# Two transformer blocks in split fp32: rows of the activations and slots of the weights 16 bytes longer

## The chip, the core and the metric

The kernel runs on one NeuronCore of a Trainium2 chip. The metric is the device time of one execution in microseconds (us). Matrix products run on TensorE (PE in the profile, its weight loads PEld), elementwise work on VectorE (DVE), ScalarE (ACT) and GpSimd (POOL); SyncE (SP) issues most DMAs. SBUF holds 128 partitions; a tensor `[P, k, t]` lies in each partition as k rows of t numbers of 4 bytes.

## What is computed

The reference chains two blocks on a stream x of 256 tokens and 1024 features, in float32:

```python
x = first_block(x, mem, ...)     # mixers of four kinds, cross-attention on mem, conv. gated FFN (2816)
return second_block(x, c, ctx, ...)
# second_block, two layers l:
x = ffn_half_step(x, mx[0:3], g_ffn1[l], ...)      # and the same for ctx
x = x + mx[5] * mixer(modulated_norm(x, ...))      # l = 0: Fourier and spatial gate; l = 1: attention over x and ctx
x = ffn_half_step(x, mx[6:9], g_ffn2[l], ...)      # and the same for ctx, in the first layer
# with
swiglu(h, w_gu, w_down) = (silu(h @ w_gate) * (h @ w_up)) @ w_down     # inner width 2752
ffn_half_step = x + 0.5 * gate * swiglu(rms_norm(x, g) * (1 + scale) + shift, ...)
```

Where x and ctx run together there are 512 tokens, elsewhere 256.

## The kernel before

**Split products.** Each product of an activation with a weight matrix is computed in three passes of a reduced-precision fp32 type (F32R, which TensorE takes in one pass at full clock). Both operands are split into a high and a low part: `w_hi` and `w_lo` for the weights, `xn_hi` and `xn_lo` for the normalised activations, `h_hi` and `h_lo` for the hidden units of the feed-forward. `three_passes` (L254) issues high by high (L258), high weights by low activations (L259) and low weights by high activations (L260). Each `matmul` call is a load of the first operand, the stationary one (128 columns), and a stream of the second, the moving one, of 256 or 512 columns. Products that are not split are plain fp32, which the profile shows as two matmul records for each call.

**Staging.** All weights are cut into chunks of at most 2048 columns by 128 partitions, 1 MB. SyncE loads them one after the other into the three slots of `raw`. For chunk g, ScalarE copies raw into `w_hi[:, g % 3]` (`split_hi`, L234), VectorE subtracts that from raw into `w_lo[:, g % 3]` (`split_lo`, L242), and TensorE waits for `lo_ready` before it uses the slot and raises `chunk_done` after it. Splits run two chunks ahead of the products.

**The loops on TensorE.** `pe_feature_major` goes through the chunks of a job; in each it goes over k (8 rows of the activations for an up or plain projection, 11 for a down projection) and within k over the output tiles n (two in general, one in the down projections). So six matmuls in a row share row k of the moving operand in an up projection, three in a down projection. A chunk is 48 matmuls in the one and 33 in the other. `win_pe` does the same for the input projections of the first block; its job `w_in_small` has one output tile. `pe_token_major` has the activations stationary and the weights moving. The job list is fixed in `plan`; the order on each engine is that of the program, with semaphores between engines.

**Where the tensors lie.** Tensors are allocated in the order in which they are named, each at the next multiple of 32 bytes: raw, w_hi, w_lo, xc, xn_hi, xn_lo, small, ident, minus, rot, row_sums, work, rstd, half, mods, gains, scales, b_mod, c_in, c_pad, mrow, and then those of a stage: z and the tables of the first block, later in the same place h_hi and h_lo, or the tensors of the two mixers of the second block. raw starts at a multiple of 64. `small` collects columns of constants and has 280 of them. `work` (8192 columns) is scratch; the feed-forward uses its columns 4096 to 7167, the norms 0 to 4095, the means of the last norm 7168 to 7679.

Of the kernel before, what the change touches and what calls it, by code (L numbers as in the profile page):

```python
# [38 lines left out]
F32 = mybir.dt.float32  # L39
F32R = mybir.dt.float32r  # L40
I32 = mybir.dt.int32
ACT = mybir.ActivationFunctionType
ALU = mybir.AluOpType
AX_X = mybir.AxisListType.X

P = 128
T = 256
D = 1024
KT = D // P
SLOTS = 3  # L50
CHUNK = 2048
EPS = 1e-6
HEADS = 4
HD = 64
FF_TILES = 22
HALF = FF_TILES // 2
# [72 lines left out]
def build(nc, io, plan):  # L129
# [23 lines left out]
    with ExitStack() as ctx:  # L153
        def sb(name, shape, dt=F32, scope=ctx):
            return scope.enter_context(nc.sbuf_tensor(name, shape, dt))
# [5 lines left out]


        raw = sb("raw", [P, SLOTS, CHUNK])
        w_hi = sb("w_hi", [P, SLOTS, CHUNK], F32R)
        w_lo = sb("w_lo", [P, SLOTS, CHUNK], F32R)
        xc = sb("xc", [P, KT, 2 * T])
        xn_hi = sb("xn_hi", [P, KT, 2 * T], F32R)
        xn_lo = sb("xn_lo", [P, KT, 2 * T], F32R)
        small = sb("small", [P, io["small"].shape[1]])
        ident = sb("ident", [P, P])  # L170
        minus = sb("minus", [P, P])
# [1 line left out]
        row_sums = sb("row_sums", [P, 32])  # L173
        work = sb("work", [P, 8192])
        nrm = work[:, 0:KT * 2 * T].rearrange("p (k t) -> p k t", k=KT)
        rstd = sb("rstd", [P, 2 * T])
        half = sb("half", [P, 2 * T])
        mods = sb("mods", [P, 144, 2])
# [2 lines left out]
        b_mod = sb("b_mod", [P, 144])  # L181
        c_in = sb("c_in", [P, KT, 2])
        c_pad = sb("c_pad", [P, KT, C_AT + 32])
        mrow = sb("mrow", [P, 256])
        X = slice(0, T)
        C = slice(T, 2 * T)
        XC = slice(0, 2 * T)
# [1292 lines left out]
            "ff_gate", "ff_hi", "ff_lo", "ff_convolved", "ff_newest_tap"))  # L1480
        later = ExitStack()
        mix.close()
        h_hi = sb("h_hi", [P, HALF, 2 * T], F32R, scope=later)
        h_lo = sb("h_lo", [P, HALF, 2 * T], F32R, scope=later)
        fbuf = [work[:, 4096 + i * 1024:4096 + (i + 1) * 1024].rearrange("p (n t) -> p n t", n=2) for i in range(SLOTS)]

        def packed(s):
# [487 lines left out]
        o_t = area(0, KT, 2 * T)  # L1975
# [64 lines left out]
        def branch_act(act, norm, then):  # L2040
            norm.act_rest(act)
            for name in L0_TABLES:
                act.dma_start(L0_TABLES[name][:], io[name]).then_inc(l0_tables_in, 16)
            run_act(act, jobs["ab_a"], act_copy_to(act, a_t, w=2 * T), counts=True)
            run_act(act, jobs["ab_v"], act_tokens_to(act, v_t, ACT.Gelu_apprx_tanh), counts=True)
            act.wait_ge(g_dve, 3)
            act.activation(vst2, vst, ACT.Abs_reciprocal_sqrt).then_inc(g_act, 1)
            run_act(act, jobs["ab_u"], act_copy_to(act, u_t, ACT.Gelu_apprx_tanh, w=2 * T), counts=True)

            def middle(j):  # L2050
                act.wait_ge(f_mid, j + 1)
                if j >= 2:
                    act.wait_ge(f_sum, j - 1)
                got, m, h = psum[:, MID_BANK + j % 2, 0:T].rearrange("p (n t) -> p n t", n=2), mid[j % 2], P // 2
                act.activation(m[:, :, 0:h + 1], got[:, :, 0:h + 1], ACT.Copy)
                act.activation(m[:, :, P + 1:P + h], got[:, :, h + 1:P], ACT.Copy)
                act.activation(m[:, :, P - 1:h:-1], got[:, :, 1:h], ACT.Copy)
                act.activation(m[:, :, 2 * P - 1:P + h:-1], got[:, :, h + 1:P], ACT.Copy, scale=-1.0).then_inc(f_mid_out, 1)

            def fourier_high(g):  # L2060
                act.wait_ge(f_sum_out, 4 * g + 4)
                act.activation(xn_hi[:, g, :], o_t[:, g, :], ACT.Copy).then_inc(o_hi, 1)

            def gated_high(i):
                act.wait_ge(g_dve, 10 + 2 * i)
                k = slice(4 + 2 * i, 6 + 2 * i)
                act.activation(xn_hi[:, k, :], o_t[:, k, :], ACT.Copy).then_inc(o_hi, 1)

            def odd_out(j):
                act.wait_ge(f_sum, j + 1)  # L2070
                if j >= 2:
                    act.wait_ge(f_sum_out, 2 * j - 2)
                act.activation(odd_half[j % 2], psum[:, TOKEN_BANK + j % 2, T:T + P + 1], ACT.Copy).then_inc(f_odd, 1)

            middle(0)
            for j in range(3):
                middle(j + 1)
                odd_out(j)
            fourier_high(0)
            middle(4)  # L2080
            odd_out(3)
            middle(5)
            odd_out(4)
            fourier_high(1)
            middle(6)
            odd_out(5)
            gated_high(0)
            middle(7)
            odd_out(6)
            fourier_high(2)  # L2090
            odd_out(7)
            gated_high(1)
            fourier_high(3)
            run_act(act, jobs["ab_out"], then.act_squares_after(act))

        def branch_dve(dve, rows_out, columns, closing):
            rows_out()
            run_dve(dve, jobs["ab_a"], None)
            columns()
            run_dve(dve, jobs["ab_v"], None)  # L2100
            n = 0

            def o(ins):
                nonlocal n
                n += 1
                ins.then_inc(g_dve, 1)
                dve.wait_ge(g_dve, n)
            v = v_t[:, :, :].rearrange("p n (g f) -> p (n g) f", f=P)
            dve.wait_ge(evacuated, jobs["ab_v"].base + 2)
            dve.wait_ge(l0_tables_in, 16 * len(L0_TABLES))  # L2110
            o(dve.tensor_tensor(vsq, v, v, ALU.mult))
            o(dve.tensor_reduce(vst3, vsq, AX_X, ALU.add))
            o(dve.tensor_scalar(vst, vst3, 1.0 / P, EPS, ALU.mult, ALU.add))
            dve.wait_ge(g_act, 1)
            o(dve.scalar_tensor_tensor(vst3, vst2, -0.5, vst2, ALU.mult, ALU.mult))
            o(dve.tensor_tensor(vst3, vst3, vst, ALU.mult))
            o(dve.scalar_tensor_tensor(vst2, vst3, 1.5, vst2, ALU.add, ALU.mult))
            o(dve.tensor_tensor(v, v, vst2.unsqueeze(2).to_broadcast([P, 16, P]), ALU.mult))
            gv = gv_row[:, :, :].unsqueeze(1).to_broadcast([P, 4, 4, P])
            v4 = v_t[:, :, :].rearrange("p n (g f) -> p n g f", f=P)  # L2120
            o(dve.tensor_tensor(v4, v4, gv, ALU.mult))
            for i in range(2):
                dve.memset(mid[i][:, :, P:2 * P:P // 2], 0.0).then_inc(f_clear, 1)
            run_dve(dve, jobs["ab_u"], None)

            def halves(j):

                dve.wait_ge(f_odd, j + 1)
                g, t = j // 2, j % 2 * T
                even, odd = psum[:, TOKEN_BANK + j % 2, 0:P + 1], odd_half[j % 2]  # L2130
                dve.tensor_tensor(o_t[:, g, t:t + P + 1], even, odd, ALU.add).then_inc(f_sum_out, 1)
                dve.tensor_tensor(o_t[:, g, t + T - 1:t + P:-1], even[:, 1:P], odd[:, 1:P], ALU.subtract).then_inc(f_sum_out, 1)

            def low(i, k):
                dve.wait_ge(o_hi, i + 1)
                dve.tensor_tensor(xn_lo[:, k, :], o_t[:, k, :], xn_hi[:, k, :].bitcast(F32), ALU.subtract).then_inc(o_lo, 1)

            def gated_sum(i):
                dve.wait_ge(g_pe, i + 1)
                gated = o_t[:, 4 + 2 * i:6 + 2 * i, :].rearrange("p g (n t) -> p g n t", t=P)  # L2140
                bs = bs_row[:, 2 * i:2 * i + 2, :].unsqueeze(2).to_broadcast([P, 2, 4, P])
                got = psum[:, GATED_BANK:GATED_BANK + 2, :].rearrange("p g (n t) -> p g n t", t=P)
                o(dve.tensor_tensor(gated, got, bs, ALU.add))

            def gated_product(i):
                k = slice(4 + 2 * i, 6 + 2 * i)
                o(dve.tensor_tensor(o_t[:, k, :], o_t[:, k, :], u_t[:, 2 * i:2 * i + 2, :], ALU.mult))

            for j in range(3):
                halves(j)  # L2150
            gated_sum(0)
            halves(3)
            gated_product(0)
            low(0, 0)
            halves(4)
            halves(5)
            low(1, 1)
            gated_sum(1)
            halves(6)
            gated_product(1)  # L2160
            low(2, slice(4, 6))
            halves(7)
            low(3, 2)
            low(4, slice(6, 8))
            low(5, 3)
            run_dve(dve, jobs["ab_out"], dve_add_gated(dve, 2, gate_of(1), 2), closing=closing.dve_last(dve, gate_of(1)))
# [45 lines left out]
        block = ctx.enter_context(nc.Block())  # L2212
# [743 lines left out]
```

## Time and profile before

| | |
|---|---|
| time, median of 3 runs | 2172.94 us (2171.1 to 2174.55) |
| span of the profiled execution | 2171.7 us |
| busy: TensorE, weight loads | 97%, 84% |
| busy: VectorE, ScalarE, GpSimd | 45%, 38%, 10% |
| granted TensorE clock, mean | 0.993 of full |
| DMA, mean | 145 GB/s |

A record of a matmul runs from its start to its modelled end, its latency included, so records of consecutive matmuls overlap. The pace of TensorE is read from the starts in the timeline. A stretch is described by its first and its last start and the number of intervals between them.

### The profile page before, as it was taken

Reading aid. Unit: us, or ns where it says so; the run is one execution under the profiler, and the core shown is the slowest. Engines: PE = TensorE matmul, PEld = TensorE weight load, DVE = VectorE, ACT = ScalarE, POOL = GpSimd, SP = SyncE. Lnnn points to the kernel's source line nnn. Section 1 sums busy time; section 2 is a strip of 40 time slices with the busy share of each in tenths; the row PEclk is TensorE's granted clock in tenths of the full one; section 3 lists DMA queues with packets and bytes.
Section 4 is the critical chain, followed back from the end, with each engine's and each line's share of the span. In section 5 each row is a group of like instructions: output and inputs, shape, how many; then the busy total and the mean of one; then the engine's idle time right before and its main releaser. Section 6 shows DMA issues by size and latency. Waiting matters only on the chain.

```text
span 2171.7 us, 31784 instructions
## 1 busy us (share of the span) xinstructions
PE 2104.7 (97%) x13882; PEld 1815.8 (84%) x13882; DVE 984.8 (45%) x1270; ACT 817.4 (38%) x1046; POOL 224.3 (10%) x185
## 2 busy tenths in 40 slices
PE   7988999999999999999999999999999999999998
PEld 6985998999878888788887888888778888869998
DVE  6768555767522322354542332243232235645444
ACT  5742455655522222244332222233222224445444
POOL 1000001413111010100101001111000110001001
PEclk9999999999999999999999999999999999999999
DMA  6425545454532333452343332243334222364453
GB/s 235 156 79 200 214 169 191 155 190 164 215 149 78 108 141 114 158 204 99 127 156 134 110 115 82 86 163 136 137 125 155 75 80 102 117 252 156 167 178 112
DMA packets 53708, 313.97 MB, mean 145 GB/s; under 512 B 5952, under 2 KB 12353, under 8 KB 23745
## 3 DMA queue, kind: packets, MB, share of 16 engines
q1 hardware_dynamic: 50848, 308.98, 39.7%
q10 hardware_dynamic: 2720, 2.95, 0.4%
q8 instruction: 109, 1.79, 0.3%
q14 instruction: 31, 0.25, 0.0%
HBM read 310.86 MB, written 1.05 MB: 144 GB/s over the span
## 4 chain that ended last, share of the span: by engine, by line
PE 86%; DVE 6%; ACT 4%; issue 3%; DMA 1%; SPq 0%; DVEq 0%; ACTq 0%
PE psum L258 26%; PE psum L260 26%; PE psum L259 26%; PE psum L1646 3%; ACT w_hi L234 2%; DVE w_lo L242 1%; PE psum L1293 1%; PE psum L1283 1%; PE psum L1307 0%; DMA raw<-in_w_in_r 0%; DVE xn_lo L1811 0%; PE psum L895 0%; PE psum L1714 0%; DVE work L1000 0%; PE psum L896 0%
## 5 line engine op out<-in xcount | busy, mean ns | idle before, releaser
L258 PE MATMUL psum<-xn_hi,w_hi 128*128 128x256 f32 (+1 forms) x2600 | 864.4, 332 | 17.5 <-DVE xn_lo L438 7.5
L259 PE MATMUL psum<-xn_lo,w_hi 128*128 128x256 f32 (+1 forms) x2600 | 853.2, 328 | 0.0
L260 PE MATMUL psum<-xn_hi,w_lo 128*128 128x256 f32 (+1 forms) x2600 | 852.8, 328 | 0.0
L242 DVE TENSOR_TENSOR w_lo<-raw,w_hi 128x2048 fp32r<-128x2048 f32 (+1 forms) x246 | 509.9, 2073 | 453.8 <-ACT w_hi L234 453.0
L258 PEld LDWEIGHTS psum<-xn_hi,w_hi 128*128 128x128 f32 x2600 | 497.0, 191 | 74.5 <-issue 23.3
L259 PEld LDWEIGHTS psum<-xn_lo,w_hi 128*128 128x128 f32 x2600 | 497.4, 191 | 43.0 <-issue 1.2
L260 PEld LDWEIGHTS psum<-xn_hi,w_lo 128*128 128x128 f32 x2600 | 497.2, 191 | 42.3
L234 ACT ACTIVATE w_hi<-raw 128x2048 fp32r<-128x2048 f32 (+1 forms) x246 | 421.7, 1714 | 216.9 <-PE psum L260 139.1
L258 PE MATMUL psum<-h_hi,w_hi 128*128 128x512 f32 (+1 forms) x913 | 314.9, 345 | 1.8 <-POOL h_lo L1621 1.7
L259 PE MATMUL psum<-h_lo,w_hi 128*128 128x512 f32 (+1 forms) x913 | 313.2, 343 | 0.0
L260 PE MATMUL psum<-h_hi,w_lo 128*128 128x512 f32 (+1 forms) x913 | 313.2, 343 | 0.0
L1621 POOL TENSOR_TENSOR h_lo<-work,h_hi 128x512 fp32r<-128x512 f32 (+1 forms) x110 | 154.4, 1404 | 1143.5 <-ACT h_hi L1553 1143.5
L1542 ACT ACTIVATE work<-psum 128x512 f32<-128x512 f32 (+1 forms) x88 | 47.9, 545 | 476.0 <-PE psum L260 476.0
L1591 DVE TENSOR_TENSOR work<-work,psum 128x512 f32<-128x512 f32 (+1 forms) x88 | 54.6, 621 | 373.0 <-ACT work L1542 373.0
L258 PEld LDWEIGHTS psum<-h_hi,w_hi 128*128 128x128 f32 x913 | 171.7, 188 | 27.0 <-issue 2.5
L259 PEld LDWEIGHTS psum<-h_lo,w_hi 128*128 128x128 f32 x913 | 171.8, 188 | 22.5
L260 PEld LDWEIGHTS psum<-h_hi,w_lo 128*128 128x128 f32 x913 | 171.8, 188 | 22.4
L1474 DVE SCALAR_TENSOR_TENSOR xc<-psum,mods,xc 128x256 f32<-128x256 f32 x126 | 55.7, 479 | 185.8 <-PE psum L260 185.5
L369 POOL TENSOR_TENSOR work<-work 128x256 f32<-128x256 f32 (+1 forms) x60 | 62.1, 1035 | 721.0 <-ACT work L360 671.6
L360 ACT ACTIVATE work<-xc 128x512 f32<-128x512 f32 (+2 forms) x42 | 26.1, 622 | 188.3 <-DVE xc L1474 167.0
L1553 ACT ACTIVATE h_hi<-work 128x512 fp32r<-128x512 f32 (+1 forms) x110 | 60.1, 546 | 81.4 <-DVE work L1591 81.4
L1646 PE MATMUL psum<-raw,c_pad 128*32 128x256 f32 x1152 | 73.6, 383 | 0.3 <-DMA raw<-in_mod 0.3
(375 smaller groups left out, 1324.4 us busy)
## 6 DMA issues: line engine op xcount, KB each, us to landing
raw<-in_mod SPq DMA_DIRECT2D x72, 1024.0 KB, 4.9
raw<-in_a_up SPq DMA_DIRECT2D x42, 1024.0 KB, 4.9
raw<-in_b_up SPq DMA_DIRECT2D x42, 1024.0 KB, 4.8
raw<-in_ffn_up SPq DMA_DIRECT2D x22, 1024.0 KB, 4.9
raw<-in_a_down SPq DMA_DIRECT2D x32, 704.0 KB, 4.1
raw<-in_b_down SPq DMA_DIRECT2D x32, 704.0 KB, 4.1
raw<-in_ffn_down SPq DMA_DIRECT2D x16, 704.0 KB, 4.2
raw<-in_wo SPq DMA_DIRECT2D x8, 1024.0 KB, 4.8
```

Of the source, the lines that this page charges most:

```text
L234: act.activation(w_hi[:, slot, 0:size], raw[:, raw_slot(("main", g)), 0:size], ACT.Copy).then_inc(hi_ready, 1)
L242: dve.tensor_tensor(w_lo[:, slot, 0:size], raw[:, raw_slot(("main", g)), 0:size], w_hi[:, slot, 0:size].bitcast(F32), ALU.subtract).then_i ...
L258: pe.matmul(out, lh, rh, start=first, stop=False, skip_group_check=group)
L259: pe.matmul(out, lh, rl, start=False, stop=False, skip_group_check=group)
L260: return pe.matmul(out, ll, rh, start=False, stop=last, skip_group_check=group)
L369: pool.tensor_tensor(nrm[:, 0, 0:self.w], nrm[:, 0, 0:self.w], nrm[:, k, 0:self.w], ALU.add).then_inc(n_added, 1)
L1474: mm = dve.scalar_tensor_tensor(x, got, gate[:, tile, h], x, ALU.mult, ALU.add)
L1542: act.activation(b[r, 0, 0:self.w], psum[r, s.bank, 0:self.w], ACT.Silu).then_inc(ff_gate, 1)
L1553: act.activation(out, b[r, 1:2, 0:self.w], ACT.Copy).then_inc(ff_hi, 1)
L1591: dve.tensor_tensor(b[r, 1, 0:self.w], b[r, 0, 0:self.w], up[up_r], ALU.mult).then_inc(evacuated, 1)
L1621: pool.tensor_tensor(lo, b[r, 1:2, 0:self.w], hi.bitcast(F32), ALU.subtract).then_inc(ff_lo, 1)
L1646: mm = pe.matmul(psum[q, 7, 0:256], c_pad[:, k, C_AT - 2 * j:C_AT - 2 * j + 32], raw[:, raw_slot(("mod", m)), k * 256:(k + 1) * 256], star ...
```

## The change

Four tensors of split operands get four more columns (16 bytes) in each row or slot. Nothing reads or writes these columns; where a whole row was addressed, a slice (`XC`, columns 0 to 511) takes its place. `small` is filled up with zero columns to a multiple of 16 columns. `mrow`, a buffer of 256 columns that turns the modulation rows into columns, is no tensor of its own any more but a part of `work`.

```diff
+ROW_PAD = 4
@@
-        w_hi = sb("w_hi", [P, SLOTS, CHUNK], F32R)
-        w_lo = sb("w_lo", [P, SLOTS, CHUNK], F32R)
+        w_hi = sb("w_hi", [P, SLOTS, CHUNK + ROW_PAD], F32R)
+        w_lo = sb("w_lo", [P, SLOTS, CHUNK + ROW_PAD], F32R)
         xc = sb("xc", [P, KT, 2 * T])
-        xn_hi = sb("xn_hi", [P, KT, 2 * T], F32R)
-        xn_lo = sb("xn_lo", [P, KT, 2 * T], F32R)
+        xn_hi = sb("xn_hi", [P, KT, 2 * T + ROW_PAD], F32R)
+        xn_lo = sb("xn_lo", [P, KT, 2 * T + ROW_PAD], F32R)
@@
         nrm = work[:, 0:KT * 2 * T].rearrange("p (k t) -> p k t", k=KT)
+        mrow = work[:, 7680:7936]
@@
-        mrow = sb("mrow", [P, 256])
@@
-        h_hi = sb("h_hi", [P, HALF, 2 * T], F32R, scope=later)
-        h_lo = sb("h_lo", [P, HALF, 2 * T], F32R, scope=later)
+        h_hi = sb("h_hi", [P, HALF, 2 * T + ROW_PAD], F32R, scope=later)
+        h_lo = sb("h_lo", [P, HALF, 2 * T + ROW_PAD], F32R, scope=later)
@@
-                act.activation(xn_hi[:, g, :], o_t[:, g, :], ACT.Copy).then_inc(o_hi, 1)
+                act.activation(xn_hi[:, g, XC], o_t[:, g, :], ACT.Copy).then_inc(o_hi, 1)
@@
-                act.activation(xn_hi[:, k, :], o_t[:, k, :], ACT.Copy).then_inc(o_hi, 1)
+                act.activation(xn_hi[:, k, XC], o_t[:, k, :], ACT.Copy).then_inc(o_hi, 1)
@@
-                dve.tensor_tensor(xn_lo[:, k, :], o_t[:, k, :], xn_hi[:, k, :].bitcast(F32), ALU.subtract).then_inc(o_lo, 1)
+                dve.tensor_tensor(xn_lo[:, k, XC], o_t[:, k, :], xn_hi[:, k, XC].bitcast(F32), ALU.subtract).then_inc(o_lo, 1)
@@
+    block("pad", np.zeros((P, -width % 16)))
```

## Rows read from the trace of the kernel before

**Rows 1.** The page's part 1: busy us, share of the span, instructions

```profile
PE 2104.7 (97%) x13882; PEld 1815.8 (84%) x13882; DVE 984.8 (45%) x1270; ACT 817.4 (38%) x1046; POOL 224.3 (10%) x185
```

**Rows 2.** The page's part 4: the chain that ended last, by line

```profile
PE psum L258 26%; PE psum L260 26%; PE psum L259 26%; PE psum L1646 3%; ACT w_hi L234 2%; DVE w_lo L242 1%; PE psum L1293 1%; PE psum L1283 1%; PE psum L1307 0%; DMA raw<-in_w_in_r 0%; DVE xn_lo L1811 0%; PE psum L895 0%; PE psum L1714 0%; 
```

**Rows 3.** Waits of TensorE: total us, times, longest us; the largest

```profile
PE psum L373 <- POOL work L369: 9.1, 1, 9.1
```

**Rows 4.** Groups by form: line engine op out<-in shapes xcount | busy us, mean ns | idle

```profile
L258 PE MATMUL psum<-xn_hi,w_hi 128*128 128x256 f32 x1520 | 442.7, 291 | 17.5 <-DVE xn_lo L438 7.5 <-DVE xn_lo L1811 4.0 <-DVE xn_lo L440 3.7
L258 PE MATMUL psum<-xn_hi,w_hi 128*128 128x512 f32 x1080 | 421.7, 390 | 0.0
L258 PE MATMUL psum<-h_hi,w_hi 128*128 128x512 f32 x495 | 196.4, 397 | 0.0
L258 PE MATMUL psum<-h_hi,w_hi 128*128 128x256 f32 x418 | 118.6, 284 | 1.8 <-POOL h_lo L1621 1.7
L258 PE MATMUL psum<-w_hi,xn_hi 128*128 128x256 f32 x160 | 46.7, 292 | 0.0
```

**Rows 5.** Timeline of TensorE: start us, us, line; 256 columns on xn, 44 rows

```profile
2009.82 0.28 PE L258 MATMUL psum<-xn_hi,w_hi 128*128 128x256 f32 x1
...
2014.98 0.28 PE L259 MATMUL psum<-xn_lo,w_hi 128*128 128x256 f32 x1
```

**Rows 6.** The same view, 512 columns on xn, 49 rows

```profile
1318.54 0.39 PE L258 MATMUL psum<-xn_hi,w_hi 128*128 128x512 f32 x1
...
1329.42 0.39 PE L258 MATMUL psum<-xn_hi,w_hi 128*128 128x512 f32 x1
```

**Rows 7.** The same view, 256 columns on h, 33 rows

```profile
535.73 0.28 PE L260 MATMUL psum<-h_hi,w_lo 128*128 128x256 f32 x1
...
539.51 0.28 PE L259 MATMUL psum<-h_lo,w_hi 128*128 128x256 f32 x1
```

**Rows 8.** The same view, 512 columns on h, 35 rows

```profile
692.01 0.40 PE L259 MATMUL psum<-h_lo,w_hi 128*128 128x512 f32 x1
...
699.94 0.40 PE L260 MATMUL psum<-h_hi,w_lo 128*128 128x512 f32 x1
```

**Rows 9.** The same view, w_in_small, 22 rows

```profile
64.19 0.28 PE L258 MATMUL psum<-xn_hi,w_hi 128*128 128x256 f32 x1
...
66.71 0.28 PE L258 MATMUL psum<-xn_hi,w_hi 128*128 128x256 f32 x1
```

**Rows 10.** The same view at the halved clock, 22 rows, and its granted clock

```profile
122.37 0.41 PE L260 MATMUL psum<-xn_hi,w_lo 128*128 128x256 f32 x1
...
126.85 0.41 PE L260 MATMUL psum<-xn_hi,w_lo 128*128 128x256 f32 x1
...
122.00:127.00 5.00, 5.00 (x24) 0.50 0.32 98
```

**Rows 11.** The same view, fp32 products of the attention, eight in one row

```profile
1898.69 1.89 PE L1293 MATMUL psum<-work,v 128*128 128x256 f32 x8
```

**Rows 12.** Instructions of line 1293: duration ns min/median/max, first and last start

```profile
L1293 PE MATMUL psum<-work,v x64: 379/379/483, 1898.7 to 1942.9; 128*128 128x256 f32 x64
```

**Rows 13.** Timeline of TensorE where 512 columns begin, rows 1, 2, 3 and 6

```profile
958.02 0.40 PE L258 MATMUL psum<-xn_hi,w_hi 128*128 128x512 f32 x1
958.25 0.40 PE L259 MATMUL psum<-xn_lo,w_hi 128*128 128x512 f32 x1
958.49 0.39 PE L260 MATMUL psum<-xn_hi,w_lo 128*128 128x512 f32 x1
...
959.18 0.39 PE L260 MATMUL psum<-xn_hi,w_lo 128*128 128x512 f32 x1
```

**Rows 14.** The same view where 256 columns begin, rows 1 and 10

```profile
2069.86 0.28 PE L258 MATMUL psum<-xn_hi,w_hi 128*128 128x256 f32 x1
...
2070.93 0.28 PE L258 MATMUL psum<-xn_hi,w_hi 128*128 128x256 f32 x1
```

**Rows 15.** Splitting on VectorE, by form; columns as in rows 4

```profile
L242 DVE TENSOR_TENSOR w_lo<-raw,w_hi 128x2048 fp32r<-128x2048 f32 x161 | 370.4, 2301 | 333.9 <-ACT w_hi L234 333.3
```

## The prediction, made before the change was run

> **What bounds the kernel now.** I read the shares first, then the clock and the chain, then the starts of single matmuls. TensorE is busy for 2104.7 of 2171.7 us, VectorE for 45% of the span and ScalarE for 38% [rows 1]. The chain that ended last lies 26% each on the lines 258, 259 and 260, the three passes of the split product [rows 2]; the longest waits of TensorE together are a few tens of us, the largest 9.1 us [rows 3]. So the time is the number of matmuls times the interval between their starts, and almost nothing else. The counts per pass are in [rows 4]: with the activations as moving operand 1520 of 256 columns and 1080 of 512, with the hidden units 418 and 495, and 160 with the weights moving. Times three passes that makes 5040 matmuls of 256 columns and 3240 of 512 on the normalised activations, 1254 and 1485 on the hidden units.
>
> The mean durations in [rows 4] are of no use for an interval, since a matmul's record covers its latency as well. The reader has to take starts. Between 2009.82 and 2014.98 us lie 43 intervals, 120.0 ns each [rows 5]; between 1318.54 and 1329.42 lie 48, 226.7 ns each [rows 6]. On the hidden units, from 535.73 to 539.51, there are 32 intervals of 118.1 ns [rows 7] and from 692.01 to 699.94 there are 34 of 233.2 ns [rows 8].
>
> **Why phase can matter at all.** These four figures differ by operand, not only by size. The code gives the addresses. All tensors up to `small` have sizes that are multiples of 64 bytes; `small` has 280 columns, 1120 bytes, so all that comes after it, h_hi and h_lo among it, starts 32 bytes beyond a multiple of 64, while xn_hi, xn_lo, w_hi and w_lo start at one. Both rows and slots are 2048 and 8192 bytes, so k and slot change nothing. Hence moving and stationary operand have the same phase where xn is used, and phases 32 apart where h is used: 226.7 against 233.2 ns at 512 columns, 120.0 against 118.1 at 256. That the down projection fills one bank while the up projections alternate between two is not the reason: w_in_small also fills a single bank and its 21 intervals from 64.19 to 66.71 are 120.0 ns each [rows 9].
>
> What the ideal is shows where the moving operand is read at half the rate. At the halved clock (granted 0.50) the 21 intervals from 122.37 to 126.85 are 213.3 ns for 256 columns, which is 256 columns at 1.2 GHz with nothing on top [rows 10]. The unsplit fp32 products of line 1293 stream at the same rate at full clock: eight last 1.89 us of which the last takes 0.379 [rows 11, 12], so 1.511/7 = 215.9 ns, 2.6 on top, although their operands have mixed phases. At full rate 256 and 512 columns last 106.7 and 213.3 ns at 2.4 GHz; the overheads are then 13.3 and 13.4 ns with equal phases and 11.4 and 19.9 with phases 32 apart. So some 9 to 17 ns of every split matmul are a stall that comes only when the moving operand is streamed at full rate beside the next weight load.
>
> The third thing to see is that the steady intervals are a state that is reached. When 512 columns begin at 958.02, the first five intervals are (959.18 - 958.02)/5 = 232.0 ns, and only then does it run at 226.7 [rows 13]; when 256 columns begin after the hidden units at 2069.86 the first nine are (2070.93 - 2069.86)/9 = 118.9 ns [rows 14], before 120.0 holds. Out of this locked state the equal phases therefore cost about the same as phases 32 apart: about 232 and 118.5.
>
> **The change, part by part.** Row k of xn_hi, xn_lo, h_hi and h_lo now lies at 16 times (k mod 4) bytes beyond a multiple of 64, slot s of the weights at 16 s. `small` grows to 288 columns (1152 bytes), and h starts at 0 instead of 32. In every chunk the difference of phase between moving and stationary operand therefore runs through 0, 16, 32 and 48 and moves on after six matmuls in the up projections (two tiles of three passes) and after three in the down projections.
>
> First the term of the order. The lock takes about five intervals to form [rows 13], and the phase moves on after three or six, so I take it that it no longer forms. For 512 columns on xn that costs 232.0 - 226.7 = 5.3 ns times 3240 = +17.2 us, less 0.5 us for the some hundred matmuls that are unlocked now (20 stretches of five). For 512 columns on h it gives (232.0 - 233.2) times 1485 = -1.8 us. For 256 columns on xn, 118.5 - 120.0 = -1.5 ns times 5040 = -7.6 us, less 0.7 that is unlocked now; on h (118.5 - 118.1) times 1254 = +0.5. The sum is 17.2 - 0.5 - 1.8 - 7.6 + 0.7 + 0.5 = +8.5 us. A sixth matmul of each six may run locked, which takes some 2 us off. I forecast +6 to +7.
>
> Then the term that the trace does not show: phases 16 and 48 apart, which half of the matmuls get. Its lower bound is the overhead of the half-rate stream, 2.6 ns [rows 11]: 109.3 and 215.9 ns, which against the forecast is (118.5 - 109.3) times 6294/2 = 29 us and (232.0 - 215.9) times 4725/2 = 38 us, together 67 us less than forecast. Its upper bound is the worst single interval shown, 240 ns in the starts of [rows 13] (958.25 to 958.49), 8 more than the forecast's; with the same 8 ns at 256 columns, 8 times (2362 + 3147) gives 44 us more. I take neither, since the two differences that are shown agree out of lock within 1.2 ns, and a difference of 16 lies between them.
>
> The skill has a rule against all of this. The Trainium skill, SBUF — State Buffer, section SBUF: two separate sides, says that only the port pair shared by VectorE and GpSimd causes contention and that TensorE never waits for anyone at its ports; TensorE: Matmul & The Clock Gate, section Step-by-step, adds that loading the next weights takes no read bandwidth from the running matmul. By these pages phase would be nothing and the change would cost nothing. [rows 6] and [rows 8] differ by 6.5 ns a matmul with the same count of columns, so the trace doesn't agree with the rule taken that far; what it would mean is the second rival.
>
> The other parts have one answer. Writers: the second half of splitting a chunk takes VectorE 2301 ns on average [rows 15], while the 48 matmuls of a chunk of 256 columns last 48 times 120, 5.76 us, so a few ns more or less of a write at phase 16 is hidden behind them; if that cover is gone, at the start of a stage, it counts. The chain has 3% in the two splits [rows 2], at the starts of stages; 1% of slower writes there is 0.6 us. `mrow` moves into columns of `work` that nothing else uses; its six copies and what waits for them stay as they are. The slices with `XC` cut the new padding off: the same elements in two runs. No instruction, DMA or wait is added on any queue; the DMA of `small` carries 32 bytes more in each of 128 rows. Identity, `minus`, `work` and z move from phase 32 to 0; their products are the half-rate ones, 2.6 ns on top whatever the phase.
>
> **The rivals.** (1) *The streams come apart, and it is faster.* If the stall is a meeting of the two read streams in the same 16 bytes modulo 64, then a difference of 16 or 48 may let one run ahead of the other without meeting. For it: the stall vanishes at half rate, and differences 0 and 32 are both even. Against: weights advance more slowly than the moving operand, so the two lap each other from any start. It decides the sign from 2 ns less in the odd rows: 2 times 5509 matmuls is 11 us, which turns +6 into -5. The full price is 67 us under the forecast, 2112; half of it, which I take, gives about 2145. (2) *Nothing changes.* The lock forms anew within a row or carries over, or the order of banks and not the phase makes the difference; time 2173. For it: 256 and 512 columns nearly cancel. (3) *Odd starts cost more*, as reads that straddle a unit of 32 bytes: up to 44 us over the forecast, 2195 at a middle price and 2222 at the full one. Nothing in the trace reads a split operand at such a start.
>
> **How the numbers follow.** The profiled span of 2171.7 us is within 1.3 us of the median, 2172.9, so I add to the median: 2172.9 + 6 = 2179. Chances: the forecast 0.42, faster by parting 0.28, nothing 0.15, odd starts cost more 0.15. A measurement can tell about 0.2%, 4.3 us, from no change. The forecast's own range, 2166 to 2190, splits into 0.09 below 2168.6, 0.13 within 0.2% and 0.20 above 2177.3. The second rival goes to no change but for 0.01. That gives faster 0.28 + 0.09 = 0.37, same 0.13 + 0.14 = 0.27, slower 0.20 + 0.15 + 0.01 = 0.36. The range leaves out the full prices of the first rival and of the third: 2132 to 2203.
>
> **What would show it.** Starts in the profile after: up chunks of 512 columns near 232 ns without runs of 226.7; chunks of 256 near 118.5; down chunks of 512 no longer in pairs of 232 and 235. If odd rows stand out within a chunk, with six intervals shorter or longer than their neighbours, the first or third rival holds, and that is what would make the prediction wrong by tens of us. If up chunks show 226.7 throughout, the lock does not depend on the difference. Busy TensorE should stay at 97%, the waits of [rows 3] as they are.

## The result, and the profile after

The changed kernel takes 2181.87 us (median of 5 runs, 2180.73 to 2184.43), the kernel before beside it 2173.32 us. The ratio is 1.0041, 95% interval 1.003 to 1.0051: slower, by 8.6 us. The forecast was 2179.0 us. The profiled execution spans 2179.1 us, 7.4 more than before.

First the shares, the chain and the longest wait of TensorE, which answer to [rows 1], [rows 2] and [rows 3]:

```profile
PE 2110.4 (97%) x13881; PEld 1809.4 (83%) x13882; DVE 985.5 (45%) x1270; ACT 818.2 (38%) x1046; POOL 225.7 (10%) x185
...
PE psum L259 26%; PE psum L260 25%; PE psum L261 25%; PE psum L1647 3%; ACT w_hi L235 2%; DVE w_lo L243 2%; PE psum L1294 1%; PE psum L1284 1%; DVE work L432 0%; PE psum L1308 0%; DMA raw<-in_w_in_r 0%; DVE xn_lo L1812 0%; PE psum L896 0%; DVE work L1001 0%; PE psum L897 0%
...
PE psum L374 <- POOL work L370: 8.8, 1, 8.8
```

Little but TensorE's own busy time moved: 2110.4 against 2104.7 us. The three passes (now lines 259 to 261) still carry the chain, and the longest wait is 8.8 us where it was 9.1. Next the groups by form, in the columns of [rows 4]:

```profile
L259 PE MATMUL psum<-xn_hi,w_hi 128*128 128x256 f32 x1520 | 440.4, 290 | 19.6 <-DVE xn_lo L439 8.7 <-DVE xn_lo L441 3.7 <-DVE xn_lo L1812 3.6
L259 PE MATMUL psum<-xn_hi,w_hi 128*128 128x512 f32 x1080 | 426.2, 395 | 0.0
L259 PE MATMUL psum<-h_hi,w_hi 128*128 128x512 f32 x495 | 195.2, 394 | 0.0
```

A record holds the latency too, but that part stays the same, so the records of the same form can be compared between two kernels: 512 columns on the normalised activations went from 390 to 395 ns, 512 on the hidden units from 397 to 394, 256 on the activations from 291 to 290. Then the starts, as in [rows 5] to [rows 8], each pair being the first and the last start of a stretch without a wait, of 74, 49, 61 and 86 intervals:

```profile
1317.63 0.39 PE L260 MATMUL psum<-xn_lo,w_hi 128*128 128x512 f32 x1
...
1334.79 0.40 PE L259 MATMUL psum<-xn_hi,w_hi 128*128 128x512 f32 x1
...
691.62 0.39 PE L261 MATMUL psum<-h_hi,w_lo 128*128 128x512 f32 x1
...
702.97 0.40 PE L259 MATMUL psum<-h_hi,w_hi 128*128 128x512 f32 x1
...
534.77 0.28 PE L260 MATMUL psum<-h_lo,w_hi 128*128 128x256 f32 x1
...
542.00 0.28 PE L261 MATMUL psum<-h_hi,w_lo 128*128 128x256 f32 x1
...
2009.81 0.28 PE L261 MATMUL psum<-xn_hi,w_lo 128*128 128x256 f32 x1
...
2019.97 0.28 PE L260 MATMUL psum<-xn_lo,w_hi 128*128 128x256 f32 x1
```

These are 231.9, 231.6, 118.5 and 118.1 ns; before they were 226.7, 233.2, 118.1 and 120.0. The 512-column products on xn lost 5 ns each, the others gained a little or stayed.

Below, an interval given for a whole kernel is the mean over all starts of its trace, with the gaps of a wait and the stretches at the halved clock left out (3214 intervals for 512 columns on xn, 1472 on h, 4361 and 1234 for 256 columns; before 226.8, 233.3, 119.9 and 118.3 ns, after 231.5, 231.7, 118.1 and 118.1). **Difference** means the address of the moving operand less that of the stationary one, modulo 256 bytes. In the kernel before it is 0 for everything on xn and 224 on h, since h starts 32 bytes lower against that unit.

### The profile page after: what moved, and what is told of

It is laid out like the page before. It is cut to its first block, busy times and chain, and to the rows that moved or that the text cites. A ratio compares the mean times of both kernels' runs of the same rounds, so it can differ in the third digit from the quotient of the medians.

```text
span 2179.1 us, 31783 instructions
## 1 busy us (share of the span) xinstructions
PE 2110.4 (97%) x13881; PEld 1809.4 (83%) x13882; DVE 985.5 (45%) x1270; ACT 818.2 (38%) x1046; POOL 225.7 (10%) x185
## 4 chain that ended last, share of the span: by engine, by line
PE 84%; DVE 7%; ACT 4%; issue 3%; DMA 1%; SPq 0%; DVEq 0%; ACTq 0%
PE psum L259 26%; PE psum L260 25%; PE psum L261 25%; PE psum L1647 3%; ACT w_hi L235 2%; DVE w_lo L243 2%; PE psum L1294 1%; PE psum L1284 1%; DVE work L432 0%; PE psum L1308 0%; DMA raw<-in_w_in_r 0%; DVE xn_lo L1812 0%; PE psum L896 0%; DVE work L1001 0%; PE psum L897 0%
## 5 line engine op out<-in xcount | busy, mean ns | idle before, releaser
L259 PEld LDWEIGHTS psum<-xn_hi,w_hi 128*128 128x128 f32 x2600 | 491.9, 189 | 80.7 <-issue 24.3
```

What stands on the lines that cost most here:

```text
L259: pe.matmul(out, lh, rh, start=first, stop=False, skip_group_check=group)
```

## The experiments

The theory on record was that equal phases lock into a steady interval, good for 512 columns (226.7) and bad for 256 (120.0), and that the change breaks the lock. The first rival is that the order of the loops or of the banks makes the difference between xn and h, and not the address.

**The hidden units alone.** The kernel before, with nothing changed but the width of `small`, which moves h by 32 bytes to a difference of 0:

```diff
+    block("pad", np.zeros((P, -width % 16)))
```

> The kernel before with nothing but `small` filled up to 288 columns: h_hi and h_lo now start at a multiple of 64 as the weights do; no row or slot is longer. Theory of the lock (equal phases let the steady interval settle at 226.7 ns for 512 columns and 120.0 for 256; a difference of 32 never settles): the down projections go from 233.2 to 226.7 and from 118.1 to 120.0, -6.5 x 1485 + 1.9 x 1254 = -7.3 us, so 0.9966 of before. Rival (the down projections are slower because they fill one bank or loop over eleven rows, not for their phase): 233.2 and 118.1 stay, 1.000. Rival (the loss of the change comes from what else moved, `small` and `work` at another phase): this kernel is slower than before by some of the 8.5 us.

Measured: 2165.8 against 2174.07 us, ratio 0.9965 (0.9952 to 0.9979). The down projections of 512 columns, 48 intervals, and their form:

```profile
692.06 0.39 PE L258 MATMUL psum<-h_hi,w_hi 128*128 128x512 f32 x1
...
702.94 0.39 PE L258 MATMUL psum<-h_hi,w_hi 128*128 128x512 f32 x1
...
L258 PE MATMUL psum<-h_hi,w_hi 128*128 128x512 f32 x495 | 193.3, 390 | 0.0
```

That is 226.7 ns and 390 ns a record, exactly what the up projections have, where it was 233.2 [rows 8] and 397. At 256 columns h now takes 120.0, like xn. So the address decides and not the order of the work, and this part of the change, undone from the rest, makes the kernel faster by 8.3 us. The intervals account for 7.7 of them: 1485 times 6.5 ns is 9.7, less 1254 times 1.6 ns, 2.0. The port rule that the prediction quoted (the Trainium skill, SBUF — State Buffer, section SBUF: two separate sides, by which TensorE never waits on anyone) doesn't foresee this: the same matmuls, 32 bytes apart, differ by 6.5 ns each. Whether that is a wait at a port isn't shown.

**Which unit the phase has.** The prediction took 64 bytes. In the first run rows of xn alone are 64 bytes longer, so that all differences on xn are multiples of 64, and h is aligned as above (`mrow` lies in `work`, as in the change):

```diff
+ROW_PAD = 16
-        xn_hi = sb("xn_hi", [P, KT, 2 * T], F32R)
+        xn_hi = sb("xn_hi", [P, KT, 2 * T + ROW_PAD], F32R)
```

> The changed kernel with rows of xn 64 bytes longer in place of 16, and no padding of the weights and of h: every operand is at phase 0. Theory of the lock: what counts is the phase modulo 64, so 226.7 and 120.0 throughout, as in the run with h aligned, 0.9966 of before. Rival (a row that is not a multiple of 2048 bytes, whatever its phase, breaks the lock): up chunks at 231.8 and 118.3 ns as in the changed kernel, about 1.000 to 1.003 of before.

Measured: 2174.71 us, 1.0008 (0.9999 to 1.0017). The theory with a unit of 64 wanted 0.9966 and fell. The rival on record, that a row which isn't a multiple of 2048 bytes breaks the lock, fits this run as well; further down rows of 2048 bytes at constant differences of 64, 128 and 192 don't run at 226.7 either, so the length of the rows isn't needed to explain it. Up projections of 512 columns, 74 intervals:

```profile
1317.64 0.39 PE L261 MATMUL psum<-xn_hi,w_lo 128*128 128x512 f32 x1
...
1334.80 0.40 PE L260 MATMUL psum<-xn_lo,w_hi 128*128 128x512 f32 x1
```

They take 231.9 ns, unlocked, while h in the same kernel runs at 226.9. The trace also tells how the lock is missed. All six matmuls of a row have one difference here, and those at difference 0 show, from the first to the sixth (means of 119 to 138 rows): 226.8, 235.2, 229.3, 231.8, 230.3, 227.0 ns. The lock is there at the sixth, and then the row ends. At a difference of 192 all six are between 233.0 and 233.4. A new stage of down projections at 0 in this kernel goes through the same five and then stays at 226.7. So what [rows 13] showed is confirmed: five intervals with a mean of about 231, though they range from 226.8 to 235.2, and then the steady one.

**The parts of the change.** The slots of the weights alone, and the rows of the activations alone, each 16 bytes longer, with `small` and `mrow` as in the change:

```diff
-        w_hi = sb("w_hi", [P, SLOTS, CHUNK], F32R)
+        w_hi = sb("w_hi", [P, SLOTS, CHUNK + ROW_PAD], F32R)
```

> The changed kernel with only the slots of the weights 16 bytes longer: within a chunk the difference of phase is constant, 0 in slot 0, 48 in slot 1, 32 in slot 2. Theory of the lock: slot 0 settles at 226.7 and 120.0, slot 2 stays at 233.3 and 118.3; slot 1 shows what a lasting difference of 48 gives, for which the changed kernel has only stretches of three to six (231.8 and 118.3). Sum with slot 1 unlocked: xn at 512 columns +4.0 x 3240, at 256 -1.1 x 5040, h at 512 -2.6 x 1485, at 256 +0.6 x 1254 = +4.3 us, 1.002 of before. Rival (an odd difference that lasts parts the two streams): slot 1 near 216 and 109 ns, some 30 us faster than that, 0.988.

> The changed kernel with only the rows of the activations 16 bytes longer: in every slot the difference runs through 0, 16, 32, 48 as k advances, just as in the changed kernel. Theory of the lock: the same as the changed kernel, 231.8 and 118.3 ns everywhere, 1.004 of before. Rival (the slots' padding, with its writes by ScalarE and VectorE at other phases, carries the loss): 1.000 to 1.002.

Measured: 1.0078 (1.0066 to 1.0091) and 1.0027 (1.0016 to 1.0038). Both parts alone cost time, and the change is not their sum. The rows alone lie between what was expected (1.004) and the rival (1.000 to 1.002); the slots alone are further off than anything expected. With the rows alone 512 columns take 231.2 ns on xn and 231.1 on h, 256 columns 118.1 and 117.4; the slots add little on top. With the slots alone the expectation was 1.002, since one slot of three was to stay locked; none does. The reason is in the addresses: w_hi is 24,624 bytes long, so w_lo and what follows move, and slot 0 stands at differences of 128 to w_hi and 64 to w_lo, which are equal only modulo 64. Two chunks of 48 matmuls, slots 0 and 2, 46 intervals each:

```profile
1138.15 0.39 PE L261 MATMUL psum<-xn_hi,w_lo 128*128 128x512 f32 x1
...
1148.88 0.39 PE L259 MATMUL psum<-xn_hi,w_hi 128*128 128x512 f32 x1
...
1304.76 0.40 PE L261 MATMUL psum<-xn_hi,w_lo 128*128 128x512 f32 x1
...
1315.40 0.39 PE L259 MATMUL psum<-xn_hi,w_hi 128*128 128x512 f32 x1
```

233.3 and 231.3 ns. Here the differences (one to w_hi, one to w_lo) repeat every three matmuls through the whole chunk, and the mean of 512 columns on xn, 232.6, is even above the 231.5 of the change. So for 512 columns it isn't the moving on from row to row that costs most, but that a difference is no longer 0. The moving operand has one address modulo 256 in all three slots, so the address of the stationary one matters too. And the interval isn't simply the mean of what its differences give when they last (table below): for slot 0, with 128 twice and 64 once, that mean is 231.4, for slot 2, with 96 twice and 32 once, 233.3, and the trace has them the other way round.

**One difference at a time.** Six kernels hold the difference constant, each with one value for xn and another for h. The tensors have their old row length and start so many bytes later (weights as before, `small` and `mrow` as in the change):

```diff
+X_AT, H_AT = 16, 32      # columns of 4 bytes: 64 and 128 bytes
+        def shifted(name, k, at, room, scope=ctx):
+            flat = sb(name, [P, k * 2 * T + room], F32R, scope=scope)
+            return flat[:, at:at + k * 2 * T].rearrange("p (k t) -> p k t", k=k)
```

> Rows and slots as in the kernel before (no padding), but xn_hi and xn_lo start 64 bytes further from the weights and h_hi and h_lo 128 further, modulo 256. The run with rows 64 longer did not lock although every difference was 0 modulo 64, so the unit must be larger. If the unit is 128 bytes: h at 128 locks (226.7 and 120.0 ns), xn at 64 does not (about 232 and 117 to 118). If it is 256: h at 128 is unlocked as well (232, 118). If it is 64 after all and the length of the rows broke the lock: both lock. Times in that order: 0.997 + 1.005 - 1 = about 1.003 of before; 1.005; 0.997.

> The same with xn 32 and h 16 bytes further. Theory (only a difference of zero locks at 226.7; any other costs about 232 and 118 ns, as in the changed kernel): xn 232 and 118, h 232 and 118; +5.3 x 3240 - 1.7 x 5040 = +8.6 us, 1.003. Rival (some lasting difference parts the two read streams): one of the four intervals is under 224 or under 115 ns.

> The same with xn 80 and h 112 bytes further. Theory as for 32 and 16: 232 and 118 ns, 1.003 of before. Rival: a lasting odd multiple of 16 parts the streams, under 224 or under 115 ns.

> The same with xn 48 and h 192 bytes further. With a unit of 128, h at 192 is the same as xn at 64 in the run before last, and both intervals must agree with those; with a unit of 256 they may differ. xn at 48 by the theory 232 and 118, 1.003 of before; by the rival under 224 or 115 ns.

> The same with xn 96 and h 144 bytes further: neighbours of 112. The theory of the changed kernel (any difference but zero gives 232 and 118): 1.004 of before. Rival (a difference that lasts has an interval of its own, and 112 is the bottom of a slope): h at 144 or xn at 96 between 114 and 117 ns at 256 columns, under 231 at 512.

> The same with xn 240 and h 160 bytes further. 240 is 128 away from 112. If the unit were 128 for all but the locked state, xn at 240 would give 113.8 and 228.6 as h at 112 does, about 0.986 of before; if the unit is 256 it gives another value, by the theory of the changed kernel about 118 and 232, 1.004.

Single times, beside 2172.85 us for the kernel before: 2168.84, 2182.42, 2171.21 and 2188.8; beside 2175.16: 2191.62 and 2194.14. The ratios, 0.998, 1.004, 0.999, 1.007, 1.008 and 1.009, are of single times. The intervals of all differences tried, in ns (those at 0 and 224 from the kernel before, at 112 from this group and the next run):

| difference, bytes | 512 columns | 256 columns |
|---|---|---|
| 0 | 226.8 | 119.9 |
| 16 | 231.7 | 117.3 |
| 32 | 233.3 | 117.0 |
| 48 | 232.6 | 118.4 |
| 64 | 229.1 | 117.2 |
| 80 | 231.1 | 119.3 |
| 96 | 233.3 | 119.9 |
| 112 | 228.6 to 230.6 | 113.8 to 114.1 |
| 128 | 232.5 | 118.7 |
| 144 | 233.3 | 118.4 |
| 160 | 234.3 | 117.8 |
| 192 | 233.3 | 116.7 |
| 224 | 233.3 | 118.3 |
| 240 | 236.0 | 117.2 |

Against what was expected: only the run with 32 and 16 came out as the theory said. That with 64 and 128 matched none of its three cases, since 128 doesn't lock and 64 has an interval of its own. 112 on h gave the rival's interval under 115 ns. 192 on h differs from 64 on xn, and 240 on xn from 112 on h, so the unit isn't 128. 48, 96, 144, 240 and 160 gave nothing under 115 or 224 ns, and their kernels were slower than the 1.003 to 1.004 expected. That every difference but 0 costs about 232 and 118 is therefore wrong as well.

Three of them in the timeline: 512 columns at 64 (48 intervals, 229.0 ns), 256 columns at 112 (63 intervals, 113.3 ns) and 256 columns at 96 (68 intervals, 120.0 ns):

```profile
1317.79 0.39 PE L263 MATMUL psum<-xn_lo,w_hi 128*128 128x512 f32 x1
...
1328.78 0.39 PE L263 MATMUL psum<-xn_lo,w_hi 128*128 128x512 f32 x1
```

```profile
534.77 0.28 PE L263 MATMUL psum<-h_lo,w_hi 128*128 128x256 f32 x1
...
541.91 0.28 PE L263 MATMUL psum<-h_lo,w_hi 128*128 128x256 f32 x1
```

```profile
2009.74 0.28 PE L262 MATMUL psum<-xn_hi,w_hi 128*128 128x256 f32 x1
...
2017.90 0.28 PE L264 MATMUL psum<-xn_hi,w_lo 128*128 128x256 f32 x1
```

The differences 0, 64, 128 and 192 give four different values, so the unit is larger than 128 bytes; 256 fits all that was run. By the sizes of the tensors h in the first experiment lies 256 bytes beyond a multiple of 512 from the weights and xn at one, and both take 226.8 ns and 119.9 to 120.0, so for a difference of 0 a larger unit is unlikely; for the others it isn't excluded. A difference of 0 is the best of all for 512 columns and, with 96, the worst for 256. The plain means of the table, one value for each difference, are 232.2 and 117.9 ns. The changed kernel, which walks through all multiples of 16, has 231.5 to 231.7 and 118.1.

At the halved clock nothing of this is left. 256 columns at a difference of 112 and at one of 96, which take 113.3 and 120.0 ns at full clock, 24 and 23 intervals, each with its stretch's granted clock (0.50) from the view by windows:

```profile
1974.90 0.41 PE L264 MATMUL psum<-xn_hi,w_lo 128*128 128x256 f32 x1
...
1980.02 0.41 PE L264 MATMUL psum<-xn_hi,w_lo 128*128 128x256 f32 x1
...
1974.70:1980.00 5.30, 5.30 (x26) 0.50 0.20 85
```

```profile
20.79 0.42 PE L263 MATMUL psum<-xn_lo,w_hi 128*128 128x256 f32 x1
...
25.70 0.41 PE L262 MATMUL psum<-xn_hi,w_hi 128*128 128x256 f32 x1
...
20.80:25.90 5.10, 5.10 (x25) 0.50 1.00 377
```

213.3 and 213.5 ns, as at a difference of 0 [rows 10]; the longest such stretch of each kernel here has a mean between 212.8 and 213.6.

**All at 112.** The value that was best at 256 columns, on xn and on h:

```diff
+X_AT, H_AT = 28, 28
```

> Rows and slots as in the kernel before, xn_hi, xn_lo, h_hi and h_lo all 112 bytes further than the weights modulo 256. In the run with h at 112 the down projections ran at 113.8 ns for 256 columns and 228.6 for 512, under anything seen elsewhere at 256. If the difference alone sets the interval, xn takes the same values: (113.8 - 119.9) x 4560 + (228.6 - 226.8) x 3240 + (228.6 - 233.3) x 1485 + (113.8 - 118.3) x 1254 = -27.8 + 5.8 - 7.0 - 5.6 = -34.6 us, 0.984 of before, about 2138. Rival (113.8 belongs to the loop of the down projections, with one tile and eleven rows): xn stays at 117 to 119 at 256 columns, 0.997 to 1.000.

Measured: 2163.15 us, 0.9949 (0.9936 to 0.9963), where 0.984 was expected. 256 columns came out at 114.1 and 113.8. 512 columns took 230.3 and 230.6, more than the 228.6 that h had at this difference in the kernel with 80 and 112; on xn that alone is 11.3 us more than in the kernel before. There are two steady states at this difference, and in the stretches I read a chunk changes from one to the other at a longer gap between chunks and not within a chunk. Two chunks of the same up projection, 44 and 39 intervals:

```profile
596.94 0.39 PE L264 MATMUL psum<-xn_hi,w_lo 128*128 128x512 f32 x1
...
606.91 0.39 PE L263 MATMUL psum<-xn_lo,w_hi 128*128 128x512 f32 x1
...
642.80 0.39 PE L262 MATMUL psum<-xn_hi,w_hi 128*128 128x512 f32 x1
...
651.82 0.39 PE L262 MATMUL psum<-xn_hi,w_hi 128*128 128x512 f32 x1
```

226.6 and 231.3 ns. A second part went into waits for the low halves of the weights, which follow this sentence for the kernel before and for this one:

```profile
PE psum L258 <- DVE w_lo L242: 1.3, 1, 1.3
```

```profile
PE psum L262 <- DVE w_lo L246: 5.6, 15, 1.4
```

The intervals are 27.9 us less together, the longer gaps between split matmuls 13.7 us more (4.3 of that these waits) and all the rest of the span 6.8 us more, which leaves the 7.4 us of the spans. (Where the record of a matmul is missing, two intervals count as a longer gap, so the first two of these numbers are exact only together.)

**Two views.** xn and h are flat tensors with two views, 112 bytes apart. Stages of 256 columns use the one at 112 (except the first block's up projections and some small ones), those of 512 the one at 0:

```diff
+        def two_views(name, k, scope=ctx):
+            flat = sb(name, [P, k * 2 * T + 64], F32R, scope=scope)
+            return [flat[:, at:at + k * 2 * T].rearrange("p (k t) -> p k t", k=k) for at in (0, SHIFT)]
+        (xn_hi, xs_hi), (xn_lo, xs_lo) = (two_views(x, KT) for x in ("xn_hi", "xn_lo"))
+                self.hidden = (h_hi, h_lo) if w > T else (hs_hi, hs_lo)
```

> Each product gets the difference of address between its moving and its stationary operand (modulo 256 bytes) that was best for its size so far. xn and h are flat tensors with two views, one 112 bytes beyond the other. The stages of 256 columns (the first block without its feed-forward, wo2, and the feed-forwards of 256 tokens) use the views at a difference of 112; those of 512 columns use those at 0, and the first block's up projections too. Rows and slots have their old lengths. Theory (each difference has its own steady interval, independent of the rest of the kernel): 512 columns keep 226.8 ns on xn and get 226.8 on h instead of 233.3 (-9.7 us over 1485 matmuls); 256 columns go from 119.9 to about 113.6 on xn where they lie at 112 (2736 matmuls, -17.2 us) and from 118.3 to about 113.8 on h (-4.5 us). The intervals together would be 31 us less; of the 38 us that the intervals at 112 throughout were to give only some 12 came out as time, since matmuls then wait for the splits more often, so I expect between half and nine tenths of the 31 us here: a ratio of 0.987 to 0.993. Rival (the gain at 112 is used up by waits for the low halves of the weights, so that only the aligned hidden units remain): 0.995 to 0.9965, as when only these are aligned.

(The 38 us in this text are 34.6 in the expectation of the run before, and 27.9 of them were measured in the intervals.)

Measured: 2151.5 against 2174.23 us, 0.9897 (0.9881 to 0.9914), inside the expected 0.987 to 0.993; faster than both kernels, by 22.7 us than before. Its page, 256 columns on xn (90 intervals), 256 and 512 columns on h (63 and 49), and the waits for the splits:

```profile
PE 2075.1 (97%) x13881; PEld 1795.1 (84%) x13882; DVE 984.5 (46%) x1270; ACT 817.5 (38%) x1046; POOL 224.8 (10%) x185
...
2009.80 0.28 PE L264 MATMUL psum<-xn_hi,w_lo 128*128 128x256 f32 x1
...
2020.00 0.28 PE L264 MATMUL psum<-xn_hi,w_lo 128*128 128x256 f32 x1
...
534.78 0.28 PE L262 MATMUL psum<-h_hi,w_hi 128*128 128x256 f32 x1
...
541.92 0.28 PE L262 MATMUL psum<-h_hi,w_hi 128*128 128x256 f32 x1
...
691.70 0.39 PE L264 MATMUL psum<-h_hi,w_lo 128*128 128x512 f32 x1
...
702.81 0.39 PE L262 MATMUL psum<-h_hi,w_hi 128*128 128x512 f32 x1
...
PE psum L262 <- DVE w_lo L246: 2.2, 5, 1.4
```

113.3, 113.3 and 226.7 ns. Summed over the trace the intervals are 31.9 us less than before, the longer gaps 3.7 us and the rest 4.7 us more: 23.5 of the span's 23.4. In this run the price of a difference holds whatever the other stages do, which is what it was to tell apart: chunks at 112 settle at 113.3, chunks of 256 columns left at 0 at 120.0, and 512 columns at 226.7.

## Why the prediction was right, step by step

The result lies 2.9 us above the forecast, and slower as forecast. Part of that is luck, as the terms show. The sum of 8.5 us that the steps gave, before a locked sixth matmul was taken off, would have been 2181.4. Term by term, with the time between starts of all split products (waits among them) from the two traces:

| term | predicted, us | measured, us |
|---|---|---|
| 512 columns on xn | 17.2 - 0.5 = +16.7 | 733.3 to 748.3: +15.0 |
| 512 columns on h | -1.8 | 345.4 to 343.1: -2.3 |
| 256 columns on xn, weights moving included | -7.6 + 0.7 = -6.9 | 624.4 to 618.9: -5.5 |
| 256 columns on h | +0.5 | 154.2 to 154.0: -0.2 |
| sum | +8.5 | +7.0 |
| all else in the span | 0 | +0.4 |

**What bounds the kernel** held in the main: 7.0 of the 7.4 us by which the profiled span grew lie between starts of split products, and the splits took as long as before (2302 ns for a chunk against 2301 in [rows 15]). But not all of it is the steady interval. With the mean intervals before and after and the number of intervals, the four terms are +15.0, -2.3, -9.0 and -0.3 us, together +3.4. The other 3.6 us are longer gaps in the stages of 256 columns: 135 intervals at the pace of the halved clock (200 to 230 ns) where there were 113, and 25 gaps of over 400 ns where there were 18. Such time was not in the prediction.

**The signs and the sizes** held: up projections near 232 ns without runs of 226.7, chunks of 256 columns near 118.5, down projections no longer in their old pattern. The 118.5 was less than the 118.9 that [rows 14] give, and 118.1 was measured; the extra saving and the longer gaps nearly cancel, so the -6.9 came close to the -5.5 partly by luck. The 2 us taken off for a locked sixth matmul had no ground: in the changed kernel w_lo and xn_lo lie at other addresses modulo 256 than w_hi and xn_hi, so the difference changes from pass to pass within a row too. Without it the forecast would have been nearer.

**The lock** held as a thing that takes about five intervals to form [rows 13]: the six of the 64-byte run show it directly. As the cause of the 5 ns it is only a part. In that run the lasting values of its four differences have the mean (226.8 + 229.1 + 232.5 + 233.3) / 4 = 230.4, and 231.9 was measured. So 3.6 of the 5.1 ns come from leaving 0, whatever the order, and 1.5 from never settling. In the changed kernel the plain mean over the differences (232.2 and 117.9) already comes within 0.7 ns of what was measured, and how much of it is unsettled stays open. The mean is no rule: with the slots alone it would be 231.8 and 117.5 on xn, and 232.6 and 119.0 were measured.

**The modulus of 64** was wrong. That it did no harm here is luck: a walk through 0, 16, 32 and 48 modulo 64 is also one through the multiples of 16 modulo 256, and two values shown (0 and 224) happened to give a fair unlocked mean. It was the step that made two later expectations fail, for the 64-byte rows and for slot 0 of the weights alone. That half of the matmuls get "odd" differences unlike all that the trace showed was then no class of its own: 16, 48 and 80 lie among the others.

**The rivals.** That the streams come apart (the first) is half true. At a lasting difference of 112 the interval of 256 columns falls to 113.3, 6.6 above 106.7. But it isn't the 16 bytes as such, it doesn't come with 512 columns beyond the 226.7 already known, and a kernel that changes its difference every six or three matmuls gets something near the mean. That nothing changes (the second) fell with the order of banks: the hidden units lock as soon as they are aligned. Odd starts that cost more (the third) show nowhere in the changed kernel as rows that stand out by more than a few ns; the dearest lasting difference, 240, is 236.0.

## What to carry to other kernels

Where TensorE streams split fp32 products back to back, read the interval from the starts for each pair of operands and each size, and look at the addresses before the loops: here 32 bytes in an unrelated table of constants were worth 8.3 us, and two views 112 bytes apart, the aligned hidden units among them, 22.7. Choose one difference for each size and hold it through a stage; a pad that varies it from row to row bought about the average here. A tensor's start depends on the sizes of all before it, so after any change of one the starts have to be looked at anew.

## What was unexpected

- The interval of one and the same matmul ranges from 226.7 to 236.0 ns at 512 columns and from 113.3 to 120.0 at 256, with nothing changed but the two operands' addresses. The two sizes don't want the same difference.
- Several steady states exist at one difference: at 112 chunks of 512 columns run at 226.7 or 231.1, at 64 chunks of 256 at 113.3 or 117.8, at 80 at 118.3 or 120.0. With few exceptions each lasts through a chunk. What picks one wasn't found.
- At the halved clock nothing of this is seen at any difference. The plain fp32 products [rows 11] have only 2.6 ns on top, but no run changed the difference between their operands. So I take it for a meeting of two reads, of the moving operand and of the next weights. That is argued and not shown: no run here took the weight loads away.
- Both addresses play a part. In the token-major products the weights are the moving operand, at one address modulo 256 in every kernel with the old slots, and the activations are stationary: with xn 64 bytes further their chunks take 113.3 or 117.8 ns, the two states that h has at the same difference of 192. At 144, though, they take 120.0 where h takes 118.4. So that the difference alone counts, and not both addresses, is shown only as far as these runs go.
